# Routing each token tile inside the attention stage of a hybrid attention and expert layer

## What is computed

```
h = rms_norm(x, g_norm_mix) * (1 + sc_a) + sh_a
proj = h @ w_in                      # q latent 256, kv latent 128, rotary key 32, gMLP u and v 512 each
att = attention(8 heads, block-causal in chunks of 64)      # prompt tile t sees 128 (t + 1) keys
gm = u * spatial_gating(v)
x = x + gt_a * (concat(rms_norm(att), rms_norm(gm)) @ w_out)
h = rms_norm(x, g_norm_ffn) * (1 + sc_m) + sh_m
p_group = softmax(h @ w_router_group + b)                   # 4 groups, the best one is taken
logit_e = (h @ w_router_expert + b)[that group]             # 8 experts in it, the best two
weight = g_prob * e_prob / sum(e_prob)
y[token] += weight * (silu(h @ w_gate[e]) * (h @ w_up[e])) @ w_down[e]    # 32 experts, width 256
x = x + gt_m * y
```

## Time and profile before

| | |
|---|---|
| three runs | 1218.41, 1222.95, 1224.72 us (median 1222.95) |
| the profiled execution's own time | 1218.23 us |
| its span, first to last instruction | 1216.5 us |
| mean granted TensorE clock | 0.937 |
| busy: TensorE, VectorE, ScalarE, POOL | 88%, 52%, 22%, 27% of the span |
| attention of the prompt tiles | 416.5 to 722.7 us |
| last tiles' rows and routing | 722.7 to 803 us |

### The profile page before, as it was taken

The page is one execution under the profiler, slowest core; times in us unless marked ns, Lnnn a source line. Parts: engine busy times, 40 slices in busy tenths (PEclk is TensorE's granted clock), DMA queues, the critical chain, the costliest instruction groups (busy, mean ns, idle before and its releaser), DMA issues.

```text
span 1216.5 us, 13997 instructions
## 1 busy us (share of the span) xinstructions
PE 1069.6 (88%) x4732; PEld 688.8 (57%) x4732; DVE 629.5 (52%) x1212; ACT 267.9 (22%) x595; POOL 322.5 (27%) x352
## 2 busy tenths in 40 slices
PE   4599999999387898999999997269999999999992
PEld 1245555554155355566676764257777777777771
DVE  2445555555435355665666654744445445445442
ACT  1133222221042222322323210101121121111110
POOL 1122222222231011101101000113554454454452
PEclk9799999999669999999999998559999999999996
DMA  9964444431151033322302114825999999999940
GB/s 325 332 264 149 154 156 150 146 125 57 49 169 61 19 103 130 148 87 70 138 29 103 70 36 173 362 98 191 341 358 335 344 368 338 354 348 341 346 162 13
DMA packets 75951, 229.32 MB, mean 189 GB/s; under 512 B 27747, under 2 KB 31478, under 8 KB 60150
## 3 DMA queue, kind: packets, MB, share of 16 engines
q1 hardware_dynamic: 48464, 198.48, 43.6%
q0 software_dynamic: 24048, 26.81, 6.5%
q10 hardware_dynamic: 3382, 3.32, 0.8%
HBM read 201.09 MB, written 88.25 MB: 238 GB/s over the span
## 4 chain that ended last, share of the span: by engine, by line
PE 76%; DVE 12%; issue 3%; ACT 3%; DMA 2%; POOL 2%; ACTq 1%; DVEq 0%; POOLq 0%; SPq 0%
PE bank L902 15%; PE bank L1177 10%; PE bank L1179 9%; PE bank L1194 9%; PE bank L1060 9%; PE bank L857 8%; PE bank L1011 5%; PE bank L1036 4%; PE bank L983 2%; PE bank L885 2%; DVE probT L1771 1%; PE bank L1082 1%; POOL st L716 1%; PE bank L869 1%; PE bank L912 1%
## 5 line engine op out<-in xcount | busy, mean ns | idle before, releaser
L902 PE MATMUL bank<-W_in,hT 128*128 128x512 f32 (+3 forms) x432 | 181.8, 574 | 3.4 <-ACTq L1293 3.4
L715 POOL TENSOR_SCALAR st<-st 128x1 f32<-128x1 f32 (+6 forms) x77 | 17.7, 230 | 611.3 <-DVEq L1489 611.3
L1060 PE MATMUL bank<-W_out,mT 128*128 128x512 f32 (+1 forms) x288 | 138.7, 614 | 2.9 <-DVEq L1483 2.9
L902 PEld LDWEIGHTS bank<-W_in,hT 128*128 128x128 f32 (+1 forms) x432 | 79.9, 187 | 94.9 <-issue 89.3
L1177 PE MATMUL bank<-WG,xT 128*128 128x256 f32 x528 | 122.4, 386 | 1.3 <-ACT xT L1433 0.8
L1194 PE MATMUL bank<-WD,hidT 128*128 128x512 f32 x264 | 120.6, 600 | 2.9 <-DVE hidT L1984 2.9
L1179 PE MATMUL bank<-WU,xT 128*128 128x256 f32 x528 | 119.3, 379 | 0.0
L1179 PEld LDWEIGHTS bank<-WU,xT 128*128 128x128 f32 x528 | 100.3, 190 | 13.6
L1177 PEld LDWEIGHTS bank<-WG,xT 128*128 128x128 f32 x528 | 99.7, 194 | 14.7 <-ACT xT L1433 1.2
L1036 PEld LDWEIGHTS bank<-vall,probT 128*128 128x128 f32 (+1 forms) x656 | 78.0, 187 | 23.1 <-issue 18.4
L1771 DVE COPY probT<-bank 128x512 f32<-128x512 f32 (+3 forms) x104 | 57.0, 548 | 64.9 <-PE bank L857 57.2
(11 more groups left out here) (277 smaller groups left out, 1419.2 us busy)
## 6 DMA issues: line engine op xcount, KB each, us to landing
WG<-in_w_gate_e SPq DMA_DIRECT2D x33, 1024.0 KB, 7.2
WU<-in_w_up_e SPq DMA_DIRECT2D x33, 1024.0 KB, 9.6
WD<-in_w_down_e SPq DMA_DIRECT2D x33, 1024.0 KB, 12.1
ada_w<-in_w_ada SPq DMA_DIRECT2D x24, 1024.0 KB, 7.3
residual_scratch<-x_att SPq DMA_DIRECT2D x32, 512.0 KB, 4.3
kbuf<-k_scratch SPq DMA_DIRECT2D x12, 384.0 KB, 5.3
xbuf<-in_x_prompt SPq DMA_DIRECT2D x8, 512.0 KB, 3.5
W_in<-in_w_in SPq DMA_DIRECT2D x2, 2048.0 KB, 18.4
```

The source lines that it names most:

```text
L902: ins = mm(ps[:R, 0:n], hT[:, t % 2, k, :R], W_in[:, k, c0:c0 + n], start=(k == 0), stop=(k == KD - 1))
L1060: ins = mm(psum[6][:R, :], mT[:, k, :R], W_out[:, k, half * 512:(half + 1) * 512], start=(k == 0), stop=(k == KD - 1))
```

## The change

The order of the work is moved so that each tile is routed two tiles later, beside its heads:

- The router works on the residual instead of the normalised input. A piece `fold` (s = 1, h = 2) multiplies the modulation into the router's weights once (`w2_r`, `rb`); the transposes `x2T` of tile s - 2 stand at h = 3, the router at h = 4; the norm's root is multiplied in afterwards.
- Behind the router, at h = 4, VectorE runs `pick_experts` (24 instructions: the best group, the best two experts) and then `ffn_rows` (the two large operations of the former `tail_norm`), at h = 6 `place_tokens` (20 instructions: rank in the expert, slot, weight), at h = 7 the additions of `table`. TensorE has `rank` (2 matmuls) at h = 6 and `table` (4) at h = 7. ScalarE takes two exponentials (`router_exponentials`) behind `prep`.
- The residual is added half by half, its squares are summed by halves, and the root is made for each tile (`tail`) on POOL.
- The barrier `s_end2` and the batched routing are gone. Expert weights of slots 0 and 1 are loaded after the last head, those of 2 and 3 after the last W_out and the second gather; ScalarE's queue stores the last two tiles' rows.
- The overflow block is worked out beside the first eight expert blocks, VectorE piece by piece, TensorE (36 issues as before) in block 6.

The core of the diff:

```diff
@@ -450,34 +483,53 @@
         work = []
         if s == 0 and h in (2, 3):
             work += [("vectors", h - 2, 0)]
+        if s == 1 and h == 2:
+            work += [("fold", 0, 0)]
         if s >= 2 and h < 3:
             work += [("W_out", s - 2, 4 + h)]
+        if s >= 2 and h == 3:
+            work += [("x2T", s - 2, 0), ("x2T", s - 2, 1)]
         if s and h == 3:
             work += [("mT", s - 1, 0)]
...
         if s and h >= 4:
             work += [("W_out", s - 1, h - 4)]
+        if s >= 2 and h == 4:
+            work += [("router", s - 2, 0), ("router", s - 2, 1)]
         if s >= 2 and h == 6:
-            work += [("h2T", s - 2, 0)]
+            work += [("rank", s - 2, 0)]
         if s >= 2 and h == 7:
-            work += [("router", s - 2, 0)]
+            work += [("table", s - 2, 0), ("table", s - 2, 1)]
         if s < LAST and h == 5:
             work += [("prep", s + 1, 0)]
...
+    closing = [("W_out", LAST - 1, i) for i in range(4, 7)] + [("mT", LAST, 0), ("W_out", LAST, 0)]
+    closing += [("x2T", LAST - 1, 0), ("x2T", LAST - 1, 1), ("W_out", LAST, 1), ("router", LAST - 1, 0), ("router", LAST - 1, 1)]
+    closing += [("W_out", LAST, 2), ("W_out", LAST, 3), ("rank", LAST - 1, 0), ("W_out", LAST, 4), ("x2T", LAST, 0), ("W_out", LAST, 5)]
+    closing += [("table", LAST - 1, 0), ("table", LAST - 1, 1), ("router", LAST, 0), ("W_out", LAST, 6)]
+    closing += [("x2T", LAST, 1), ("router", LAST, 1), ("rank", LAST, 0), ("table", LAST, 0), ("table", LAST, 1)]
...
+        sp.wait_ge(s_heads, LAST + 1)
+        for b in range(2):
             load_expert(b % NG * EG + b // NG, b)
...
-        sp.wait_ge(s_tab, 1)
+        sp.wait_ge(s_y, 2 * (LAST + 1))
+        sp.wait_ge(s_xg[1], 16)
+        for b in range(2, SLOTS):
+            load_expert(b % NG * EG + b // NG, b)
...
+        def x2T_(s, half):
             t = seq[s]
             R = ROWS[t]
...
+            pe.wait_ge(s_x2, 2 * s + half + 1)
+            ps = b2.claim(pe, (f"x2T{half}", t))
+            for j in range(4):
+                ins = tr(ps[:, j * P:j * P + R], x_att[:R, s % 2, (4 * half + j) * P:(4 * half + j + 1) * P], R)
+            b2.full(ins, (f"x2T{half}", t))
...
+        def router(s, half):
+            t = seq[s]
+            R, v = ROWS[t], prompt_or_sample(t)
+            pe.wait_ge(s_x2T, 2 * s + half + 1)
+            if half == 0:
+                if s == 0:
+                    pe.wait_ge(s_w2, 1)
+                ps = b2.claim(pe, ("rt", t))
+            else:
+                ps = b2.tiles[b2.at[("rt", t)][0]]
+            for k in range(4 * half, 4 * half + 4):
+                ins = mm(ps[:R, 0:NG + NE], x2T[:, k, :R], w2_r[:, v, k, :], start=(k == 0), stop=(k == KD - 1))
+            if half:
+                b2.full(ins, ("rt", t))
+        def rank_(s):
             t = seq[s]
             R = ROWS[t]
...
+            pe.wait_ge(s_E, s + 1)
+            ps = b2.claim(pe, ("rank", t))
+            mm(ps[:R, 0:NE], tri[:R, :R], Et[:R], start=True, stop=True)
+            b2.full(mm(ps[:, NE:2 * NE], ones[:R, :], Et[:R], start=True, stop=True), ("rank", t))
+        def table(s, part):
+            t = seq[s]
+            R = ROWS[t]
+            pe.wait_ge(s_hot, 2 * s + part + 1)
+            ps = b2.claim(pe, (f"tab{part}", t))
+            src, n = ((Bv, NE), (Bw, 2 * NE))[part]
+            for k in range(2):
+                ins = mm(ps[:, 0:n], slot[:R, k, :], src[:R, k, :], start=(k == 0), stop=(k == 1))
+            b2.full(ins, (f"tab{part}", t))
+        def fold():
+            pe.wait_ge(s_wr, 64)
+            for v in range(2):
+                ps = b2.claim(pe, ("rb", v))
+                for k in range(KD):
+                    ins = mm(ps[:, 0:NG + NE], modT[:, 24 + k, v:v + 1].broadcast_to([P, P]), w_r[:, k, :], start=(k == 0), stop=(k == KD - 1))
+                b2.full(ins, ("rb", v))
...
+        for b in range(2 * SLOTS):
+            hT4(b)
+            if b == 6:
+                overflow_tables()
+            gu(b + 1, (b + 1) % SLOTS, 48 * ((b + 1) // SLOTS + 1))
+            xT4(b + 2, b % 2, 16 * ((b + 2) // 2 + 1))
+            down(b, b % SLOTS)
...
+    def router_exponentials(act, s, do):
         R = ROWS[seq[s]]
-        act.wait_ge(s_x2, s + 1)
-        do(nc.scalar.activation(junk2[:R], x_att[:R, s % 2], ACT.Square, scale=D ** -0.5, accum_out=st2[:R, 40:41]), sig[id(s_x2sq)])
+        act.wait_ge(s_rx, s + 1)
+        do(nc.scalar.activation(gneg[:R], Lt[:R, 0:NG], ACT.Exp, bias=st3[:R, 4:5], accum_out=st3[:R, 6:7]))
+        do(nc.scalar.activation(st3[:R, 7:8], st3[:R, 5:6], ACT.Exp))
...
         def residual(s, half):
-            R = ROWS[seq[s]]
+            R, p = ROWS[seq[s]], s % 2
...
             do(V.tensor_tensor(tmp2[:R, c], psum[6][:R], rows_of(s)[0][:R, c], ALU.mult))
             signal(s_yfree)
-            if half:
-                dve.wait_ge(s_ld2["x"][s % 2], 16 * (s // 2 + 1))
-                do(V.tensor_tensor(x_att[:R, s % 2], x_att[:R, s % 2], tmp2[:R], ALU.add))
-                signal(s_x2)
-        def tail_norm(s):
-            R = ROWS[seq[s]]
-            dve.wait_ge(s_x2sq, s + 1)
-            rstd()
-            do(V.scalar_tensor_tensor(tmp2[:R], x_att[:R, s % 2], st2[:R, 41:42], rows_of(s)[1][:R], ALU.mult, ALU.mult))
+            if half == 0:
+                dve.wait_ge(s_ld2["x"][p], 16 * (s // 2 + 1))
+            do(V.tensor_tensor(x_att[:R, p, c], x_att[:R, p, c], tmp2[:R, c], ALU.add))
+            signal(s_x2)
...
+        def first_max(dst, vals, n, m, R):
+            do(V.tensor_reduce(m, vals, AXX, ALU.max))
+            do(STT(qv[:R, 0:n], vals, m, desc[:R, 0:n], ALU.is_equal, ALU.mult))
+            do(V.tensor_reduce(st3[:R, 8:9], qv[:R, 0:n], AXX, ALU.max))
+            if dst is None:
+                do(TS(gneg[:R], qv[:R, 0:n], st3[:R, 8:9], NEG, ALU.not_equal, ALU.mult))
+            else:
+                do(TS(dst, qv[:R, 0:n].rearrange("p (g e) -> p g e", e=EG), st3[:R, 8:9], None, ALU.is_equal))
+        by_group = lambda ap: ap.rearrange("p (e g) -> p g e", g=NG)
+        def pick_experts(s):
+            t = seq[s]
+            R, v = ROWS[t], prompt_or_sample(t)
+            ps = b2.read(dve, ("rt", t))
+            dve.wait_ge(s_tr, s + 1)
+            last_read(STT(Lt[:R], ps[:R, 0:NG + NE], st2[:R, 48 + s % 2:49 + s % 2], rb[:R, v], ALU.mult, ALU.add), ("rt", t), b2)
+            first_max(None, Lt[:R, 0:NG], NG, st3[:R, 0:1], R)
+            do(TT(lem[:R].rearrange("p (g e) -> p g e", e=EG), Lt[:R, NG:].rearrange("p (g e) -> p g e", e=EG),
+                  bcast(gneg[:R].unsqueeze(2), [R, NG, EG]), ALU.add))
+            first_max(by_group(E1[:R, t]), lem[:R], NE, st3[:R, 1:2], R)
+            lem3 = lem[:R].rearrange("p (g e) -> p g e", e=EG)
+            do(STT(lem3, by_group(E1[:R, t]), NEG, lem3, ALU.mult, ALU.add))
+            first_max(by_group(E2[:R, t]), lem[:R], NE, st3[:R, 2:3], R)
+            do(TT(Et[:R], E1[:R, t], E2[:R, t], ALU.add))
+            signal(s_E)
+            do(TS(st3[:R, 4:5], st3[:R, 0:1], -1.0, None, ALU.mult))
+            do(TT(st3[:R, 5:6], st3[:R, 2:3], st3[:R, 1:2], ALU.subtract))
+            signal(s_rx)
+            for k, E in enumerate((E1, E2)):
+                do(TS(Bv[:R, k], E[:R, t], vtok[:R, t:t + 1], None, ALU.mult))
+            for k, E in enumerate((E1, E2)):
+                do(V.tensor_tensor_reduce(qv[:R], E[:R, t], iota_f[:R, 0:NE], 1.0, 0.0, ALU.mult, ALU.add, ecol[:R, k, t:t + 1]))
...
+        def ffn_rows(s):
+            R, p = ROWS[seq[s]], s % 2
+            dve.wait_ge(s_x2sq, 2 * (s + 1))
+            do(STT(xs[:R], x_att[:R, p], st2[:R, 48 + p:49 + p], rows_of(s)[1][:R], ALU.mult, ALU.mult))
             if s:
                 dve.wait_ge(s_st2["h2"], 16 * s)
-            do(V.tensor_tensor(perm(h2[:R]), tmp2[:R].rearrange("p (q k) -> p q k", k=KD), rows_of(s)[2][:R].rearrange("p (q k) -> p q k", k=KD), ALU.add))
+            do(TT(perm(h2[:R]), xs[:R].rearrange("p (q k) -> p q k", k=KD), rows_of(s)[2][:R].rearrange("p (q k) -> p q k", k=KD), ALU.add))
             signal(s_h2)
...
+        def place_tokens(s):
             t = seq[s]
             R = ROWS[t]
...
+            ps = b2.read(dve, ("rank", t))
+            do(TT(rankb[:R], ps[:R, 0:NE], cnt[:R], ALU.add))
+            for k, E in enumerate((E1, E2)):
+                do(V.tensor_tensor_reduce(qv[:R], E[:R, t], rankb[:R], 1.0, 0.0, ALU.mult, ALU.add, rank[:R, k, t:t + 1]))
+            for k in range(2):
+                do(TS(slot[:R, k], iota_f[:R], rank[:R, k, t:t + 1], None, ALU.is_equal))
+            signal(s_hot)
+            last_read(TT(cnt[:], cnt[:], ps[:, NE:2 * NE], ALU.add), ("rank", t), b2)
+            key = st3[:R, 10:12]
+            do(TS(key, rank[:R, :, t], P - 0.5, float(2 * NE), ALU.is_gt, ALU.mult))
+            do(TT(key, key, ecol[:R, :, t], ALU.add))
+            do(TT(st3[:R, 12:13], st3[:R, 10:11], st3[:R, 11:12], ALU.is_lt))
```

(26 more changed lines are left out.)

619 lines of the change are left out of this document (322 added, 297 removed).

## The result

The changed kernel took 1318.51 us (median of 4 runs, 1312.53 to 1321.21) against 1220.68 for the kernel before on the same chip: 1.080 times the time, 95% interval 1.074 to 1.086. The prediction was 1263, with a range of 1215 to 1290. The sign was right, the size was not: 98 us more, where 40.5 had been added up.

A forecast was written before the change was run, and what follows sets the result against it. TensorE bounds the kernel, losing time only at the boundary between attention and experts. -27 (boundary) + 3.9 (block 6) + 4 (fold) + 59.6 (tiles) = +40.5 us on 1218.2 gives 1258.7, at the median 1263; range 1215 to 1290.

The forecast's parts named there:

- The place of the cost: Tiles s = 2 to 8: routing pieces ahead of copies that TensorE needs make it wait; 59.6 us in all.
- the step on head 4: pick_experts and ffn_rows precede the probabilities' copy, so key transposes wait 4.3 us at s = 5, 27.1 over six tiles.
- the wait for x2T: Head 3 of the seven tiles: x2T copies stand before mT's, 0.7 us a tile, 4.9 in all.
- heads 6 and 7: place_tokens before the probabilities' copy, table additions and TensorE's extra short issues, less growing cover: 22.9 us over seven tiles.
- Each stall costs a spell at the lower clock too: Rival: tile stalls at six places each put some 5 us of work at half speed; +15 us, 1278; chance 0.12.
- the term of 3.9 us: Expert loop: the 36 overflow table matmuls in block 6 cost 3.9 us at full clock, VectorE's pieces fitting its idle time.
- The end of the bound, 8.7: Upper end for the block 6 table matmuls, from their 8.74 us at half clock.
- The fold: Tile s = 1, head 2: multiplying the modulation into the router's weights costs 4 us, ends 2 and 8.
- The boundary: Last head's end to first gate matmul: 62 us instead of 88.9, -27; under 55 or over 70 is wrong.
- The replay: Closing list timed from the last head's end with priced pieces: router at 16.3, ids at 53.4 us.
- The weights of blocks 2 and 3: Issued after the second gather, landing 14.8 us later, with block 2's gate work 22.9 us after issue: no wait.
- The first rival: Routing slips into VectorE's idle 14.3 us a tile, tiles grow 0.7 us each; 1209 us; chance 0.20.

The follow-up runs named there:

- run 3: Changed kernel with all but the first operation of pick_experts, and ffn_rows, moved behind head 5's copies, ScalarE's exponentials one head later; 1283.02 us.
- run 2: Changed kernel with 16 matmuls that nobody reads put ahead of the next tile's key transposes in tiles 2 to 8; 1308.76 us.
- run 8: Run 6's kernel with three more places changed in the tiles and a closing list where last-tile W_out continues while VectorE routes the tile before; 1232.92 us.
- Run 1: Changed kernel with the 36 overflow table matmuls moved from the head of block 6 to the head of block 7; 1306.47 us.
- Run 6: Changed kernel with overflow tables in block 7, pick_experts, ffn_rows, place_tokens and table pieces later, first-half x2T earlier, fold at s = 2, head 0; 1261.72 us.
- runs 1 to 10: The ten follow-up kernels built on the changed kernel, with pieces reordered or unread matmuls added; measured between 1232.92 and 1308.76 us.

## Why the prediction was right or wrong

- **The place of the cost: right.** The four numbers of the step on head 4 (pick 5.3, rows 3.3, the copy behind them, a wait of 4.3) were measured as 5.6, 3.2 and 4.46 us, the wait of all six tiles as 26.1 for 27.1, and run 3, which changes that place and little else, took 35 us away. TensorE's idle time in the tiles grew by 46 us; the sum had some 55 for waits. This total is nearer than its parts: the wait for x2T was 10.0 us where 4.9 had been put for head 3, heads 6 and 7 had 5.3 and 8.2 where 22.9 stood with some 5 of issues in it.
- **The clock: the step that failed.** "Each stall costs a spell at the lower clock too" stood as a rival with +15 us and a chance of 0.12. Every tile has a clock under 1.00, and the slower work costs about 44 us (52.8 us of busy time less 9.0 of new issues). Two errors made it small: it was counted at six places, where the seven tiles have 29 waits of 0.9 us or more, with a lower clock behind 20 of them, and it was written as a case beside the forecast, though it follows from the forecast's own stalls. Runs 2, 3 and 8 show the link: clock and busy time come back when the idle time goes, and in 3 and 8 about as much of one as of the other. The trace of the kernel before had shown such a spell, 0.68, around a wait of 1.4 us. The Trainium skill (TensorE: Matmul & The Clock Gate, what's actually happening) says that the default state is throttled and that activity releases it; the trace agrees for the waits of 4.46 and 2.22 us shown above, with 0.50 behind each.
- **Block 6: the term of 3.9 us measured 15.** It took the upper clock without a look at what stands ahead of the tables. VectorE's piece of block 5 was rightly found to fit in the idle time of VectorE, but that idle time comes after the additions, 5.2 us too late for TensorE, and behind the wait the work ran at the lower clock: 5.2 + 8.4 + 1.4 for the gate matmuls. Run 1 took 8.9 of it back. The end of the bound, 8.7, was worked out for the matmuls and had no wait in it. The stage as a whole grew less, 12.0, since block 0's gate matmuls, 6.50 us before, took 3.72.
- **The fold: 4 predicted, 6.2 measured.** Same error: s = 1 had a clock of 0.83 before and 0.73 after, and 32 issues at the lower level are 7 us. Run 6 confirms it.
- **The boundary: -27 predicted, -18 measured,** 70.7 us, beyond the 70 that the prediction had named as wrong. The replay had full speed on TensorE; the clock there is 0.73. The first 12 W_out matmuls took 7.75 us, not 5.2, the router of the tile before the last was done at 20.4, not 16.3, and the ids at 61.2, not 53.4. The order of the closing list was taken as given; run 8 shows that 10 us hang on it.
- **The weights of blocks 2 and 3: right,** no wait for them shows; block 2's gate matmuls begin without one, at 921.70 us.
- **The first rival, that the routing slips into the idle time of VectorE: wrong for this change, right as a possibility.** Run 8 has the same VectorE work in tiles that are 69 us shorter in all (336.1 against 405.1); 30 us over the kernel before remain, more than half of it busy time of TensorE.
- Not tried by itself: how much slower work each of the waits at heads 3, 6 and 7 brings. That the end of s = 0 comes 2.5 us later (388.1 us) needs no cause: in the profiles of runs 1 to 10, whose code up to there is the same, it lies between 385.1 and 388.2.

## What to carry to other kernels

Where one engine waits for another inside a stage that runs at full clock, price the wait and the work behind it: here 46 us of waits went with 44 us of slower work. When small operations are put on an engine that has idle time, ask which copy stands behind them in its queue and who holds a bank for it; the same 9 us a tile cost 14 us or 4, by place. And before work is spread over a stage, see whether only its first result is needed early: ids alone, made first, gave 0.6% without touching the tiles.
